# Five dot products of the first modulation split between GpSimd and ScalarE, the first layer's gate folding moved to the start, and the sums of x squared moved into the gate chain

## What is computed

```python
c_act = jax.nn.silu(c)
for l in range(DEPTH):                                   # DEPTH = 2
    mod = c_act @ w_ada[l] + b_ada[l]                    # 6 * 1024 values
    sh_mix, sc_mix, gt_mix, sh_mlp, sc_mlp, gt_mlp = split(mod, 6)
    h = rms_norm(x, g_pre_mix[l]) * (1 + sc_mix) + sh_mix
    y = mixer(h, w_in[l], ...)
    x = x + gt_mix * rms_norm(y, g_post_mix[l])
    ...
# in the mixer: u = h @ w_in; x_m, z, glu_a, glu_b = split(u, 4)
#   q, k from x_c = silu(short_conv(x_m)); v = x_m @ w_v
#   gates = concat(q, k, v) @ w_gates + b_gates        # 4 heads, input and forget gate
#   a = long_conv(glu_a * sigmoid(glu_b))              # 31 taps
```

## Time and profile before

| | |
|---|---|
| median of 3 runs | 2027.92 us (2026.99 to 2028.9) |
| the profiled execution | 2027.99 us, span 2026.2 us |
| busy: TensorE, VectorE, ScalarE, GpSimd | 92%, 52%, 25%, 16% of the span |
| chain that ended last | TensorE 57%, transfers 20%, VectorE 18%, ScalarE 3% |
| instructions | 20909 |

### The profile page before, as it was taken

One profiled execution on the slowest core, in us unless ns is written; L12 is line 12 of the kernel. 1 busy time (PEld: TensorE's weight loads), 2 busy tenths in 40 slices (PEclk: granted clock), 3 DMA queues, 4 the chain that ended last, 5 costly groups with the idle time before them and its releaser, 6 DMA issues.

```text
span 2026.2 us, 20909 instructions
## 1 busy us (share of the span) xinstructions
PE 1866.7 (92%) x8020; PEld 1381.0 (68%) x8020; DVE 1056.6 (52%) x2575; ACT 505.3 (25%) x1226; POOL 323.8 (16%) x341
## 2 busy tenths in 40 slices
PE   6999999999999999999999999998888887887777
PEld 5877788888887788888888787885343342443332
DVE  6996665401797422001201432236867677767755
ACT  2043221111214222110012545121322222222223
POOL 1000001000000000000000000013443444444441
PEclk9999999999999999999999999999999999998999
DMA  9614469844352143449552323529999999999996
GB/s 397 262 55 159 186 253 422 343 157 150 134 209 81 64 182 134 159 153 208 218 199 99 116 101 117 216 110 422 421 421 421 421 421 421 421 421 422 420 421 277
DMA packets 72435, 517.39 MB, mean 255 GB/s; under 512 B 8208, under 2 KB 8464, under 8 KB 11664
## 3 DMA queue, kind: packets, MB, share of 16 engines
q0 software_dynamic: 46384, 330.85, 40.7%
q1 hardware_dynamic: 25952, 185.21, 24.1%
HBM read 510.78 MB, written 5.24 MB: 255 GB/s over the span
## 4 chain that ended last, share of the span: by engine, by line
PE 57%; DMA 20%; DVE 18%; ACT 3%; issue 1%; POOL 1%; DVEq 0%; SPq 0%; POOLq 0%; ACTq 0%
DMA region<-in_peer_uv,small 18%; PE pj L624 12%; PE pj L887 10%; PE pj L902 9%; DVE region L1713 9%; PE st L1170 6%; PE pj L830 5%; DVE region L2125 2%; PE pj L637 2%; PE pj L931 1%; PE pj L1141 1%; DMA ring<-in_ring_w 1%; PE st L1089 1%; PE ms L830 1%; PE pj L922 1%
## 5 line engine op out<-in xcount | busy, mean ns | idle before, releaser
L1170 PE MATMUL st<-region 128*128 128x512 f32 x940 | 453.3, 631 | 111.5 <-ACT region L1549 111.5
L1170 PEld LDWEIGHTS st<-region 128*128 128x128 f32 x940 | 182.3, 200 | 361.7 <-issue 189.3
L624 PE MATMUL pj<-hT,ring 128*128 128x256 f32 x1760 | 385.0, 380 | 1.0 <-ACT region L1353 1.0
L2125 DVE CUSTOM_DVE_ANT_0 region<-region 128x1024 f32<-128x1024 f32 x235 | 287.3, 1224 | 163.7 <-DMA region<-in_peer_uv,small 161.3
L624 PEld LDWEIGHTS pj<-hT,ring 128*128 128x128 f32 x1760 | 332.6, 190 | 47.1 <-ACT region L1353 1.8
L528 POOL DMA_INDIRECT region<-in_peer_uv,small x235 | 259.4, 1104 | 393.6 <-PE st L1170 322.4
L887 PE MATMUL pj<-region,ring 128*128 128x256 f32 x1024 | 222.0, 379 | 0.5 <-DMA ring<-in_ring_w 0.5
L887 PEld LDWEIGHTS pj<-region,ring 128*128 128x128 f32 x1024 | 194.3, 190 | 28.0 <-DMA ring<-in_ring_w 0.9
L1549 ACT ACTIVATE region<-ident,small 128x128 f32<-128x128 f32 x256 | 89.2, 394 | 456.1 <-DVE small L2133 456.1
L1713 DVE SCALAR_TENSOR_TENSOR region<-region,pc 128x255 f32<-128x255 f32 (+19 forms) x528 | 202.6, 462 | 0.0
L1664 DVE TENSOR_TENSOR tmp<-xT,hT 128x256 f32<-128x256 f32 x32 | 13.6, 425 | 359.1 <-ACT hT L1249 359.1
(11 more groups left out here) (382 smaller groups left out, 1987.0 us busy)
## 6 DMA issues: line engine op xcount, KB each, us to landing
ring<-in_ring_w SPq DMA_DIRECT2D x157, 1024.0 KB, 4.8
region<-in_ada_rest POOLq DMA_DIRECT2D x40, 1024.0 KB, 12.4
region<-in_ada_first SPq DMA_DIRECT2D x8, 1024.0 KB, 18.6
region<-in_wqkv SPq DMA_DIRECT2D x2, 3072.0 KB, 12.1
region<-in_wcmp POOLq DMA_DIRECT2D x2, 2048.0 KB, 9.9
bias_dram<-region POOLq DMA_DIRECT2D x1, 4096.0 KB, 46.0
region<-in_w_o POOLq DMA_DIRECT2D x4, 1024.0 KB, 7.1
region<-in_peer_uv,small POOLq DMA_INDIRECT x235, 17.0
```

The costliest lines, as they stand in the source:

```text
L624: i = nc.tensor.matmul(b[:, m, :], w[:, k, P * m:P * m + P], hT[:, k, :], start=(k == 0), stop=(k == CT - 1))
L1170: i = nc.tensor.matmul(acc[:, u % 2, 512 * hf:512 * hf + 512], diag[:, m % NDIAG, :], uv[m % NBUF][:, D + 512 * hf:D + 512 * hf + 512], st ...
L2125: nc.vector.tensor_tensor_reduce(row, row, h_tok[:, u % 2, :], 1.0, 0.0, ALU.mult, ALU.add, dots[:, u, k:k + 1]).then_inc(sem("u_used"), 1)
```

## The change

Three things change in the first layer; the second layer is as before.

1. In pairs 3 to 7 VectorE keeps the dot of the shift row alone. GpSimd multiplies the scale row with `c_act` (128x1024, in place), and ScalarE sums the product with a copy that has an accumulator output, ahead of adding the shift of the tile before.
2. `wvT` and `wg` of layer 0 are loaded early, between `cols` and `ada2`; `wvT` lies where `wqkv` is loaded later. The 16 products of `fold_gates` stand ahead of `wide_first`, and ScalarE keeps them behind `finish_h`.
3. The 16 sums by token stand in place of the six `keep_awake` products in the gate chain, and VectorE waits for them and reduces them before its last five taps.

```diff
-EARLY = ["ada0", "x", "ada1", "cols", "ada2", "ring", "ada3", "ring", "ada4", "ada5", "ada6", "ada7", "ring", "ring"]
+SHARED = 3
+EARLY = ["ada0", "x", "ada1", "cols", "wv", "ada2", "ring", "ada3", "ring", "ada4", "ada5", "ada6", "ada7", "ring", "ring"]
...
-        wvT = tmp[:, :, :]
+        wvT = [wqkv[:, 0], tmp[:, :, :]]
...
+                elif what == "wv":
+                    sp.dma_start(wvT[0], a["wvT"][0].rearrange("p (c d) -> p c d", d=DH)).then_inc(sem("wg_in"), 16)
+                    sp.dma_start(wg[:, :, :], a["wg"][0]).then_inc(sem("wg_in"), 16)
...
-            pool.wait_ge(sem(f"ada_first{PAIRS - 1}"), 16)
+            pool.wait_ge(sem("c_ready"), 1)
+            for j in range(SHARED, PAIRS):
+                pool.wait_ge(sem(f"ada_first{j}"), 16)
+                nc.gpsimd.tensor_tensor(ada_first[:, j, 1, :], ada_first[:, j, 1, :], c_act, ALU.mult).then_inc(sem("c_and_products"), 1)
...
-            for s in range(2):
-                for c in range(CT):
-                    i = nc.tensor.matmul(ms[0][:, 0, CT * s + c:CT * s + c + WIDE], tmp[:, c, P * s:P * s + P], ones[:, 0:WIDE], start=True, stop=True)
-            i.then_inc(sem("x_summed"), 1)
...
                 if l == 0:
+                    for c in range(2 * H):
+                        fold_gates(l, c)
                     wide_first(W_IN_ORDER[:2])
                     wide("w_in", l, W_IN_ORDER[2:10])
...
                     wide("w_in", l, [4])
-                    keep_awake(st[:, 0, :], 6)
+                    for s in range(2):
+                        for c in range(CT):
+                            i = nc.tensor.matmul(st[:, 0, CT * s + c:CT * s + c + WIDE], tmp[:, c, P * s:P * s + P], ones[:, 0:WIDE], start=True, stop=True)
+                    i.then_inc(sem("x_summed"), 1)
...
+                    if l == 0 and shift == 0 and SHARED <= c + 1 < CT:
+                        act.wait_ge(sem("c_and_products"), 16 + c + 2 - SHARED)
+                        nc.scalar.activation(ada_first[:, c + 1, 1, :], ada_first[:, c + 1, 1, :], ACT.Copy,
+                                             accum_out=mod_sum[:, PAIRS + c + 1:PAIRS + c + 2]).then_inc(sem("x_and_sums"), 1)
                     act.wait_ge(sem("h_scaled"), h_tiles)
...
-                for m in range(2):
+                for m in range(1 if j >= SHARED else 2):
                     ada_tile(ada_first[:, j, m, :], PAIRS * m + j)
...
+                if c >= SHARED:
+                    dve.wait_ge(sem("x_and_sums"), 16 + c - SHARED + 1)
+                    dve.sem_inc(sem("ada_used"), 1)
+                    ada_at += 1
                 dve.wait_ge(sem("ada_used"), 2 * c + 2)
...
                 if l == 0:
+                    dve.wait_ge(sem("x_summed"), 2)
+                    invs += 1
+                    link_to(nc.vector.tensor_reduce(x_sum, st[:, 0, 0:2 * CT].rearrange("p (s c) -> p s c", c=CT), AX.X, ALU.add), "x_sum_kept", invs)
                     long_conv(l, 3, range(KC - 5, KC))
```

More of the change, by code:

```diff
@@ L663, in wide_first, with fold_gates @@
                         step(1, late)
+            def fold_gates(l, c):
+                if c == 0:
+                    pe.wait_ge(sem("wg_in"), 48 * l + (48 if l else 32))
+                    if l:
+                        pe.wait_ge(sem("x_sum_kept"), 1)
+                h, d = divmod(c, 2)
+                for e in range(2):
+                    i = nc.tensor.matmul(ms[0][:, 0, 32 * d + 8 * h:32 * d + 8 * h + 8], wvT[l][:, 2 * h + e, P * d:P * d + P], wg[:, 4 + e, 8 * h:8 * h + 8],
+                                         start=(e == 0), stop=(e == 1))
+                if c == 2 * H - 1:
+                    i.then_inc(sem("wvg_made"), 1)
             for l in range(DEPTH):
                 if l == 0:
+                    for c in range(2 * H):
+                        fold_gates(l, c)
                     wide_first(W_IN_ORDER[:2])
@@ L671, in _ @@
                     wide("w_in", l, W_IN_ORDER[:10], 16 * l)
-                def fold_gates(c):
-                    if c == 0:
-                        pe.wait_ge(sem("wg_in"), 48 * (l + 1))
-                        pe.wait_ge(sem("x_sum_kept"), 1)
-                    h, d = divmod(c, 2)
-                    for e in range(2):
-                        i = nc.tensor.matmul(ms[0][:, 0, 32 * d + 8 * h:32 * d + 8 * h + 8], wvT[:, 2 * h + e, P * d:P * d + P], wg[:, 4 + e, 8 * h:8 * h + 8],
-                                             start=(e == 0), stop=(e == 1))
-                    if c == 2 * H - 1:
-                        i.then_inc(sem("wvg_made"), 1)
                 drained = bank
@@ L1264, in keep_mem, with keep_fold @@
                 return nc.scalar.copy(dst, st[:, 0:2, :])
+            def keep_fold(l):
+                act.wait_ge(sem("wvg_made"), l + 1)
+                nc.scalar.copy(wvg, ms[0][:, 0, 0:64]).then_inc(sem("wvg_kept"), 1)
             for l in range(DEPTH):
@@ L1268, in _ @@
                 if l == 0:
+                    keep_fold(l)
                     nc.scalar.activation(gsum[:, 0:1], eps_col[:, :], ACT.Sigmoid)
@@ L1282, in _ @@
                         drain_u(l, W_IN_ORDER[11:12])
-                        act.wait_ge(sem("wvg_made"), l + 1)
-                        nc.scalar.copy(wvg, ms[0][:, 0, 0:64]).then_inc(sem("wvg_kept"), 1)
+                        if l:
+                            keep_fold(l)
                     if h:
@@ L1791, in _ @@
             dve.wait_ge(sem("params_in"), 16)
-            dve.wait_ge(sem("x_in"), 16)
+            dve.wait_ge(sem("x_and_sums"), 16)
             first_h(0)
```

25 lines of the change are left out of this document (12 added, 13 removed).

## The result

| | before | after |
|---|---|---|
| median of 5 runs | 2028.9 us (2026.99 to 2029.05) | 2036.99 us (2035.5 to 2039.3) |
| the profiled execution | 2027.99 us, span 2026.2 | 2036.88 us, span 2035.1 |
| mean granted clock | 0.985 | 0.982 |

The ratio is 1.0047, with a 95% interval of 1.0036 to 1.0058: slower, by 7 to 12 us. The two medians of the table lie 8.1 us apart, a ratio of 1.0040, inside that interval. The forecast was 2037.6. The runs of the kernel after spread over 3.8 us, those of before over 2.1.

The account below looks back on a forecast made before the run. It took one chain without slack as the bound, VectorE's dots and scalings from 17 us until ScalarE and TensorE lead to the convolution. Terms 7.0 + 0.1 + 1.6 + 1.1 - 0.1 = +9.7 gave 2037.6 us, range 2031.3 to 2040.

Parts of the forecast that it names:

- Turns: First modulation, tiles 3 to 7: GpSimd's products and VectorE's two-input operations block each other both ways; +7.0 us, chance 0.62.
- TensorE's clock in the first stage: Between tiles 3 and 4 TensorE idles some 4.9 us, so its next eight records run at a slower clock; +1.6 us.
- The fold, "worth nothing": The 16 fold matmuls leave 104 to 122 us, where TensorE waits for VectorE anyway, for 16.5 us; no cost.
- Keeping the fold: ScalarE's `keep_fold` moves ahead of the table load, +0.1 us, and leaves the chain at 124 us, -0.1 us.
- Load order: `wvT` and `wg` ahead of `ada2` make later loads 2.7 us later; tile 7's pair comes at 36.6 us.
- The gate chain: Layer 0: 16 matmuls of 48 columns take 3.7 us in place of 2.59; +1.1 us, VectorE's later taps hidden.
- Side by side: Rival: GpSimd's product neither is held up nor holds up anything; convolution at 45.2 us, total 2031.2 us; chance 0.10.
- one-way: Rival: GpSimd waits for VectorE, VectorE never for GpSimd; +2.6 us, total 2031.6 us; chance 0.13.
- the short product: Rival: turns with a GpSimd product of 1.2 us; +2.5 us at tile 7, total 2031.5 us; chance 0.08.

Follow-up runs that it names:

- GpSimd reads nothing: The kernel after with each product replaced by two memsets of 128x1024, the scale's part of the modulation left out; 2032.3 us, ratio 1.0022.
- Part 1 alone: The kernel before with only the sharing of tiles 3 to 7, loads, fold and sums as before; 2032.27 us, ratio 1.0025.
- the idle products: The kernel after with single `keep_awake` products by the tiles of `w_in` 11 and 15 and four behind the first head's q; 2038.29 us, ratio 1.0057.
- nothing shared: The kernel after with all sixteen dots back on VectorE (`SHARED = 8`); 2044.0 us, or 2033.44 us when GpSimd's loads wait for the last pair.
- nothing shared and the loads held: The kernel after with `SHARED = 8` and GpSimd's four loads waiting for the last pair as before; 2033.44 us, ratio 1.0028.
- part 2 alone: The kernel after with no tile shared, GpSimd's loads held, sums at the front again and six `keep_awake` products in the gate chain; 2031.75 us, ratio 1.0018.
- the longer narrow filler alone: The kernel before with the gate chain's six idle products of 256 columns replaced by 16 of 48; 2029.73 us, ratio 1.0009.

## Why the prediction was right, and where not

The time, the sign and the mechanism that decides came out. That the number fits so closely is in part luck: in the profile, the turns were 0.8 us too dear, the first stage's clock 0.9, the gate chain 0.2, and a loss of 1.08 us was missing.

**Turns, right.** Both directions are shown: product behind dot (3.39 us), dot and small operations behind product (3.37, 2.28, 2.53), in every kernel with products, and gone when GpSimd reads nothing. No row of before showed the direction VectorE behind GpSimd, and it costs the most. By the Trainium skill's "SBUF — State Buffer", section "Who interferes with whom", the shared port is an exclusive lock, and the order of issue decides who blocks; the traces agree, with 2.0 to 2.2 us where a whole product lay in the way. One product works for 2.25 us; 2.2 was taken. By the Trainium skill's "GPSIMD Engine Reference", section 3.1, half of the 4497 ns of a two-input operation over 2048 float32 would be an estimate of 2.25 us; the trace agrees. The rows that spoke for this in the kernel before were read with the dot at 1.14 us; by the row's own length 0.94 us of it was left and not 0.86. The conclusion stands either way.

**Turns, the size.** +7.0 was forecast and +6.2 measured (last scaling over at 45.88). The hand-made order of turns let the dot of tile 4 wait behind product 4. It was the other way round: the dot was 0.04 us ahead. Part 1 alone gives +5.2, so the late loads add some 1.0, about as much as two profiles can differ by chance.

**TensorE's clock in the first stage.** +1.6 forecast, +0.7 measured: from the last scaling to the convolution it is 4.04 us against 3.33. The forecast had TensorE idle for 4.9 us ahead of tile 4. It was 1.88, since tile 3 came late too. The clock granted was 0.50 to 0.54 from 41 to 44 us and 1.00 from there on, while the last scaling was still to come, so TensorE could make up a part. The same term was 0.0 in part 1 alone, with 5.37 us of idling ahead of the last 44 records, and 1.8 with the idle products, with 4.54 us ahead of the last 32. So it hangs on where the idle time lies and not only on how long it is.

**The fold, "worth nothing": wrong.** This is the step that failed. The place that the prediction named (TensorE waits for VectorE there anyway) was right for the fold's own time. But the fold's matmuls had also made TensorE reach the first head's q later, so that it waited 0.5 us twice instead of 3.02 once, and the clock held. Without it: +1.08. Idle products in its place brought 1.2 back at that spot.

**Keeping the fold.** +0.1 ahead of the table load was 0.0: with nothing shared, the last scaling to the convolution is 3.33 to 3.34 us, as before. -0.1 near 124 us is there: with nothing shared and the loads held, the second head begins 2.50 us later than before and the third 2.39.

**Load order.** Arrivals were as worked out: GpSimd starts the products of the pairs at 24.24 and from 29.13 on, for forecast 24.3 and 29.2. The prediction measured the slack at the last pair alone (2.5 us) and so held the late loads harmless without sharing. They cost 2.5 us there. The slack has to be taken at each arrival plus the work behind it: 29.3 + 4 x 3.2 is 42.1, against 39.65, and 36.6 + 3.2 is only 39.8. In the shared kernel the sum began at tile 3's arrival, and so this mistake did not enter the number. It did enter the rivals' numbers.

**The gate chain.** +1.1 forecast, +0.92 measured. The forecast took 0.115 us a record from another stage and so 3.7 for 32; on the chain they took 3.50, 0.109 each, in place of 2.59. The taps were to be hidden with 0.3 us to spare; at the next head's scores the delay grows by 0.15, so nearly all of them are. What the forecast leaves out is the clock behind narrow products, absent in the profiled execution but seen in seven of nine profiles: 0.4 to 1.4 us on the eight records alone.

**The parts against the whole.** Part 1 alone costs 4.4, part 2 alone 3.4, the longer narrow filler alone 2.0: 9.8, against 8.9 in the profiles and 9.5 by the ratio. The fit is closer than the argument is: turns and late loads overlap, the filler's 2.0 holds a clock loss that the profile of the kernel after does not have, and part 3 itself, with VectorE's wait for the sums, was not run alone.

**Rivals.** Side by side and one-way fall with the rows of 2.28 and 3.37 us, the short product with the 2.25 us. Even side by side, in the kernel whose GpSimd reads nothing, the time was 2032.3, above that rival's 2031.2. Its convolution began 0.7 us sooner than the rival said (44.46 against 45.2), and the clock took more than that back: 0.9 us in the q and k records and 1.7 behind the narrow sums.

## What to carry to other kernels

Before work is given to GpSimd, look at what VectorE and GpSimd read from SBUF in that stretch. Here VectorE's operations had two inputs and GpSimd's products two, and the lengths added: even operations on one or two columns paid 2.0 to 2.1 us when a whole product lay in the way. GpSimd's fills, which read nothing, cost VectorE nothing. For a stream of loads, take the slack at each arrival with all the work behind it, not at the last one, and look at every queue's first load. Matmuls that lie in somebody else's wait still do something: taken out, they can leave a gap that costs the clock, as the 3.02 us here did in most profiles.

## What was not expected of the hardware

- Sixteen products of 48 columns, run back to back for 3.67 us, were followed by a granted clock of 0.76 (153 to 160 us) and eight records in 2.43 us; 3.62 us of 256-column products by 1.00 and 1.57 us.
- A gap of 3.0 us cost the clock in six of eight profiles of much the same program, and left it at 1.00 in two.
- GpSimd's memsets of 128x1024, which only write, ran beside VectorE's two-input operations with no delay on either: 0.95 us each, dots at 1.22.
- Four loads of 1024 KB started from GpSimd at 9.31 us made VectorE wait 12 us in three places for loads that SyncE had issued before or just behind them; in the same kernel with the four held back it waited 1.68 us, in one place.
